# Recurrence of a Trainium2 kernel: levels 2 to 5 of the triangular inverse on half of the columns

## The reference, cut to what matters

```
def _wkv_step(S, inp):
    r_t, w_t, k_t, v_t, a_t, b_t = inp
    sa = jnp.einsum('zbhvk,zbhk->zbhv', S, a_t)
    S = S * w_t[..., None, :] + sa[..., :, None] * b_t[..., None, :] + v_t[..., :, None] * k_t[..., None, :]
    return S, jnp.einsum('zbhvk,zbhk->zbhv', S, r_t)

def wkv_bidir(state0, scan_in):
    state, ys = lax.scan(_wkv_step, state0, scan_in)
    ys = jnp.moveaxis(ys, 0, 2)
    return state, ys[0] + ys[1][:, ::-1]
```

## Time and profile before

| | before |
|---|---|
| three runs | 4251.36, 4251.43, 4254.16 us (median 4251.43) |
| the profiled execution, first to last instruction | 4251.6 us |
| PE busy over the span | 3519.7 us (83%) |
| DVE, ACT, POOL busy | 1262.1, 816.8, 419.9 us |
| mean granted TensorE clock over the span | 0.907 |
| the stretch of the 24 rounds, 1853.3 to 2652.5 us | 799.2 us |
| in it, PE, DVE, ACT, POOL busy | 634.95, 425.37, 354.89, 292.31 us |
| in it, mean granted TensorE clock | 0.91 |

### The profile page before, as it was taken

One profiled execution on the slowest core, in us unless ns is written; L12 is line 12 of the kernel. 1 busy time (PEld: TensorE's weight loads), 2 busy tenths in 40 slices (PEclk: granted clock), 3 DMA queues, 4 the chain that ended last, 5 costly groups with the idle time before them and its releaser, 6 DMA issues. The chain is left out here.

```text
span 4251.6 us, 104941 instructions
## 1 busy us (share of the span) xinstructions
PE 3519.7 (83%) x46600; PEld 2194.1 (52%) x46600; DVE 1262.1 (30%) x2938; ACT 816.8 (19%) x1925; POOL 419.9 (10%) x466
## 2 busy tenths in 40 slices
PE   4999995999997169967877877669999946998987
PEld 2445544555554135546666667345555523464564
DVE  2131114111111440045555555541111112053263
ACT  1011001110000100034444443010000001152152
POOL 0000000000000100033333333000000000000000
PEclk7999996999998589969899899769999978999998
DMA  7741115899998432110000000359999973211110
GB/s 271 297 172 40 55 40 209 302 393 389 384 385 314 154 87 98 57 38 16 18 18 18 18 18 9 123 201 336 391 382 386 384 267 94 92 40 32 59 41 25
DMA packets 319424, 707.15 MB, mean 166 GB/s; under 512 B 26829, under 2 KB 74925, under 8 KB 318348
## 3 DMA queue, kind: packets, MB, share of 16 engines
q1 hardware_dynamic: 268036, 613.55, 39.0%
q0 software_dynamic: 13552, 46.49, 3.5%
q10 hardware_dynamic: 37400, 40.52, 2.7%
HBM read 648.20 MB, written 52.31 MB: 165 GB/s over the span
## 5 line engine op out<-in xcount | busy, mean ns | idle before, releaser
L906 PE MATMUL banks<-w_gate_up,x_turned 128*32 128x256 f32 x12288 | 697.9, 383 | 31.1 <-DMA w_gate_up<-in_moe_w_up_dram 29.7
L906 PEld LDWEIGHTS banks<-w_gate_up,x_turned 128*32 128x32 f32 x12288 | 409.7, 111 | 287.8 <-issue 46.4
L924 PE MATMUL banks<-w_down_ring,hidden_turned 128*32 128x256 f32 x6144 | 344.8, 380 | 0.0
L987 DVE TENSOR_TENSOR hidden<-silu_gate,banks 128x128 f32<-128x128 f32 x192 | 55.3, 288 | 766.2 <-ACT silu_gate L961 766.2
L924 PEld LDWEIGHTS banks<-w_down_ring,hidden_turned 128*32 128x32 f32 x6144 | 193.7, 110 | 128.0
L341 PE MATMUL banks<-const_cols,h_tokens 128*128 128x128 f32 x240 | 53.7, 402 | 234.1 <-DVE h_tokens L314 151.1
L878 POOL DMA_INDIRECT x_rows<-h_rows,cell_index x64 | 58.4, 912 | 1862.9 <-PE banks L898 993.3
L460 PE MATMUL banks<-gmlp_weights,h_turned_gmlp 128*128 128x512 f32 x384 | 174.2, 609 | 12.2 <-DMA gmlp_weights<-in_ga_w_in_dram 12.2
L961 ACT ACTIVATE silu_gate<-banks 128x128 f32<-128x128 f32 x192 | 53.3, 278 | 670.2 <-PE banks L906 670.2
L2053 POOL TENSOR_TENSOR l_quarters<-l_rows,scan_masks 128x256 f32<-128x256 f32 x240 | 146.8, 646 | 249.9 <-ACT l_rows L1973 249.9
L341 PEld LDWEIGHTS banks<-const_cols,h_tokens 128*128 128x128 f32 x240 | 45.3, 216 | 243.2 <-DVE h_tokens L314 158.2
(11 more groups left out here) (469 smaller groups left out, 5348.1 us busy)
## 6 DMA issues: line engine op xcount, KB each, us to landing
w_gate_up<-in_moe_w_gate_dram SPq DMA_DIRECT2D x70, 2048.0 KB, 20.4
w_gate_up<-in_moe_w_up_dram SPq DMA_DIRECT2D x70, 2048.0 KB, 24.7
w_down_ring<-in_moe_w_down_dram SPq DMA_DIRECT2D x70, 2048.0 KB, 21.4
u_channels<-in_ada_w_dram SPq DMA_DIRECT2D x40, 1024.0 KB, 6.8
y_rows<-y_out_rows ACTq DMA_DIRECT2D x256, 96.0 KB, 6.1
gmlp_weights<-in_ga_w_in_dram SPq DMA_DIRECT2D x8, 2048.0 KB, 8.2
ab_weights<-in_ab_w_in_dram SPq DMA_DIRECT2D x6, 2048.0 KB, 8.5
ada_first<-in_ada_w_dram SPq DMA_DIRECT2D x2, 4096.0 KB, 17.5
```

The lines of the kernel that those rows point to most:

```text
L906: last = pe.matmul(ps[strip(j), GU + g, 0:2 * FQ].rearrange("p (a c) -> p a c", a=2), xT[:, e % 2, k, strip(g)], wgu[e % 3][:, :, k, j * F ...
L924: last = pe.matmul(ps[strip(j), Y + g // 2, (g % 2) * DQ:(g % 2 + 1) * DQ], hT[:, g, strip(k)], wd[:, e % 2, k, j * DQ:(j + 1) * DQ], star ...
```

## The change

What it does:

1. In levels 2 to 5 a matmul moves only the 32 columns of each unit that can be nonzero in the off-diagonal blocks (`own_half`), where it moved 64. Loads of weights stay 64x64, and the number of matmuls stays. Level 1 keeps 64 columns.
2. ACT copies 128 elements per partition of Z in levels 2 to 5, where it copied 256, into a buffer of that level's own (`Z[n]`, the other half set to zero once, by 8 memsets of 128x256 on DVE ahead of the rounds). Level 1's step now lies in `a_and_mv`.
3. DVE adds 256 elements in levels 2 to 4, where it added 512, and 128 in level 5, where it added 256. Both sides still go in one instruction, with strided operands: runs of 4, 8, 16 and 32 elements at levels 2, 3, 4, 5.
4. X is laid out by direction first, so that the same columns serve the inverse of one direction and the transpose of the other; the masks and the order of the units in `l_rows` follow (`turned`).
5. `y_two_heads` is dropped. ACT writes the transposed Y back into `y_channels`; its wait for the earlier store moves from there to round 1, just ahead of the copy that writes `y_channels` anew, and is then for the store of two groups before.

```diff
         quarter = (at // size == to // size) & (at % size >= size // 2) & (to % size < size // 2)
         turned = (at // size == to // size) & (to % size >= size // 2) & (at % size < size // 2)
-        parts[f"q1_{n}"], parts[f"q0_{n}"] = turned, quarter
-        if n == 0:
-            parts["x0"], parts["x1"] = quarter, turned
+        parts[f"q0_{n}"], parts[f"q1_{n}"] = quarter, turned
...
     def on_scalar(self, act):
         self.wait(act, "y_turned", 1)
-        self.wait_before(act, "y_stored")
...
-        XI, XX, Z = two("inverse_of_pairs", [P, 2, 4, CHUNK]), two("inverse_both_ways", [P, 2, 4, CHUNK]), two("step", [P, 4, CHUNK])
+        XI, XX = two("inverse_of_pairs", [P, DIRS, 2, 2, CHUNK]), two("inverse_both_ways", [P, DIRS, 2, 2, CHUNK])
+        Z = {n: two(f"step{n}_", [P, 4, CHUNK]) for n in range(2, LEVELS)}
+        Z[1] = [AM[h][:, 0:2, :, :].rearrange("p u a c -> p (u a) c") for h in range(2)]
...
+        half = CHUNK // 2
+        turned = lambda z, ti: (1 - z) * 2 + ti
+        def own_half(ap, zz, n):
+            return ap.rearrange("p (b a s) -> p b a s", a=2, s=2 ** n)[:, :, zz, :]
+        def own_halves(ap, n, apart, width):
+            s = 2 ** n
+            return bass.AP(tensor=ap.tensor, offset=ap.offset, ap=[ap.ap[0], [apart + s, DIRS], [2 * s, width // (2 * s)], [1, s]])
+        packed = lambda ap, n: ap.rearrange("p (z b s) -> p z b s", z=DIRS, s=2 ** n)
...
-                            for u in range(4):
+                            for u, (z, ti) in enumerate(units):
                                 for cc in range(2):
-                                    last = pe.matmul(ps[from_row(h, cc), 4 * h + 1, u * CHUNK:(u + 1) * CHUNK], LQ[h][to_row(h, cc), n - 1, u, :],
-                                                     X[h][to_row(h, cc), 0, u, :], start=True, stop=True)
+                                    factor, x = LQ[h][to_row(h, cc), n - 1, turned(z, ti), :], X[h][to_row(h, cc), z, 0, ti, :]
+                                    if n == 1:
+                                        last = pe.matmul(ps[from_row(h, cc), 4 * h + 1, u * CHUNK:(u + 1) * CHUNK], factor, x, start=True, stop=True)
+                                    else:
+                                        sums = ps[from_row(h, cc), 4 * h + 1, u * half:(u + 1) * half].rearrange("p (b s) -> p b s", s=2 ** n)
+                                        last = pe.matmul(sums, factor, own_half(x, z, n), start=True, stop=True)
...
                                     if n < last_lv:
-                                        pe.matmul(ps[to_row(h, cc), 4 * h, u * CHUNK:(u + 1) * CHUNK], X[h][here, 1, u, :], Z[h][here, u, :], start=True, stop=True)
-                                    last = pe.matmul(ps[here, 4 * h + 1, (4 + u) * CHUNK:(5 + u) * CHUNK], Z[h][here, u, :], X[h][here, 1, u, :], start=True, stop=True)
+                                        pe.matmul(sums(to_row(h, cc), 0, own), x, own_half(step, z, n), start=True, stop=True)
+                                    last = pe.matmul(sums(here, 1, other), step, own_half(x, 1 - z, n), start=True, stop=True)
...
+                            elif n < last_lv:
+                                x = own_halves(XX[h][:, 0, 0, 0, :], n, 4 * CHUNK, 4 * CHUNK)
+                                sums = ps[:, 4 * h:4 * h + 2, 4 * CHUNK:6 * CHUNK].rearrange("p a (z c) -> p z a c", z=DIRS)
+                                step = dve.tensor_tensor(x, sums, x, ALU.add)
                             else:
-                                sums = ps[:, 4 * h + 1, high]
-                                flat = lambda X: X[h][:, 1, :, :].rearrange("p u c -> p (u c)")
-                            DVE.mark(dve.tensor_tensor(flat(XX), sums, flat(XI if n == 1 else XX), ALU.add), by_dve, f"XX{n}_{h}")
+                                x = own_halves(XX[h][:, 0, 1, 0, :], n, 4 * CHUNK, 2 * CHUNK)
+                                step = dve.tensor_tensor(x, packed(ps[:, 4 * h + 1, 4 * CHUNK:6 * CHUNK], n), x, ALU.add)
+                            DVE.mark(step, by_dve, f"XX{n}_{h}")
...
-                            ACTS.mark(copy(Z[h][:, :, :].rearrange("p u c -> p (u c)"), ps[:, 4 * h + 1, low]), by_act, f"Z{n}_{h}")
+                            if n == 1:
+                                step = copy(Z[n][h][:, :, :].rearrange("p u c -> p (u c)"), ps[:, 4 * h + 1, low])
+                            else:
+                                step = copy(own_halves(Z[n][h][:, 0, :], n, 2 * CHUNK, 2 * CHUNK), packed(ps[:, 4 * h + 1, 0:2 * CHUNK], n))
+                            ACTS.mark(step, by_act, f"Z{n}_{h}")
...
                     need("YC")
+                    if rnd == 1 and c >= 2:
+                        act.wait_ge(scan_s["y_stored"], 16 * (c - 1))
```

More of the change, by code:

```diff
@@ L1723, in recurrence @@
         prepare = [Prepare(room, prepare_s, c, sets[c % 2]) for c in range(KD)]
-        scan = [Scan(core, c, scan_s, outs[c % 2], state, f_whole, y_tokens, y_dram, 3 if c < KD - 1 else 7) for c in range(KD)]
+        scan = [Scan(core, c, scan_s, outs[c % 2], state, f_whole, y_dram, 3 if c < KD - 1 else 7) for c in range(KD)]
         nothing = iter(())
@@ L1778, in _ @@
                     wait(by_dve, DVE, "QG", 1)
-                    for u, (z, ti) in enumerate(units):
+                    for z, ti in units:
+                        u = turned(z, ti)
                         for h, cc in quads:
@@ L1810, in _ @@
                             wait(by_act, ACTS, f"Z{n}_{h}")
-                            for u in range(4):
+                            for u, (z, ti) in enumerate(units):
                                 for cc in range(2):
-                                    here = from_row(h, cc)
+                                    here, x, step = from_row(h, cc), X[h][from_row(h, cc), 1 - z, 1, ti, :], Z[n][h][from_row(h, cc), u, :]
+                                    own, other = z * 2 + ti, (1 - z) * 2 + ti
+                                    if n == 1:
+                                        pe.matmul(ps[to_row(h, cc), 4 * h, own * CHUNK:(own + 1) * CHUNK], x, step, start=True, stop=True)
+                                        last = pe.matmul(ps[here, 4 * h + 1, (4 + other) * CHUNK:(5 + other) * CHUNK], step, x, start=True, stop=True)
+                                        continue
+                                    sums = lambda rows_, side, q: ps[rows_, 4 * h + side, 4 * CHUNK + q * half:4 * CHUNK + (q + 1) * half].rearrange("p (b s) -> p b s", s=2 ** n)
                                     if n < last_lv:
-                                        pe.matmul(ps[to_row(h, cc), 4 * h, u * CHUNK:(u + 1) * CHUNK], X[h][here, 1, u, :], Z[h][here, u, :], start=True, stop=True)
-                                    last = pe.matmul(ps[here, 4 * h + 1, (4 + u) * CHUNK:(5 + u) * CHUNK], Z[h][here, u, :], X[h][here, 1, u, :], start=True, stop=True)
+                                        pe.matmul(sums(to_row(h, cc), 0, own), x, own_half(step, z, n), start=True, stop=True)
+                                    last = pe.matmul(sums(here, 1, other), step, own_half(x, 1 - z, n), start=True, stop=True)
                             PE.mark(last, products, f"XX{n}_{h}")
@@ L1856, in _ @@
                     wait(by_act, ACTS, "MV")
-                    for u in range(4):
+                    for u, (z, ti) in enumerate(units):
                         for h, cc in quads:
                             here = from_row(h, cc)
-                            last = pe.matmul(ps[row[cc], 4 * h + 1, u * P:(u + 1) * P], XX[h][here, 1, u, :],
+                            last = pe.matmul(ps[row[cc], 4 * h + 1, u * P:(u + 1) * P], XX[h][here, 1 - z, 1, ti, :],
                                              AM[h][here, u, :, :].rearrange("p a c -> p (a c)"), start=True, stop=True)
@@ L1922, in _ @@
                         dve.wait_ge(by_act, ACTS.of(f"L_{h}", R))
[L1923 removed]
+                        DVE.mark(dve.copy_predicated(XI[h][:, :, 1, :, :], both("q0_0", 2, CHUNK).bitcast(U32), by_dir(fours(ps[:, 4 * h, low]))),
                                  by_dve, f"XM_{h}")
```

20 lines of the change are left out of this document (12 added, 8 removed).

## The result

The changed kernel takes 4352.66 us (median of four runs, 4343.39 to 4360.23) against 4252.8 (4251.36 to 4254.69) for the kernel before: 1.0225 times, 95% interval 1.0204 to 1.0245. It is about 100 us slower; forecast were +64, with 4315 us.

A forecast was written before the change was run, and what follows sets the result against it. No engine is full, PE is nearest; a round is a hand-over-hand chain. Sum: 4251.6 - 9.7 (copies) - 6.6 (additions) + 0 (PE's pace) + 80 (clock) = 4315.3 us; range 4205 to 4390.

The forecast's parts named there:

- A: In the 24 rounds the clock falls further than now: 4315 us, own range 4275 to 4370; chance 0.54.
- ACT's copies: Levels 2 to 5: 192 copies shorten by 110 ns each; 71 PE waits shorten by 136 ns each, -9.7 us.
- DVE's additions: Levels 2 to 5: shorter additions, mostly under PE's other work; waits before L1860 and L1800 shrink, -6.6 us.
- PE's pace: Levels 2 to 5: loading weights, not columns, sets the matmul pace, so 32 columns save 0.
- The clock, +80: In the rounds, fewer columns keep the clock low: 200 us more at 1.2 GHz, at 0.40 each, +80 us.
- Rival C: Levels 2 to 5: columns set PE's pace after all, saving up to 92 us of matmul time; 4181 us, chance 0.12.
- B: In the rounds the clock holds at 0.91 and only shorter copies and additions count: 4235 us, chance 0.20.
- D: In the rounds gain and clock loss cancel, or strides eat the gain: 4243 to 4260 us, chance 0.14.
- The memsets, the new wait, the masks and the layout: Ahead of and within the rounds: memsets fit into slack, the awaited store is old, sizes stay; 0 us.

The follow-up runs named there:

- the run with 96: Changed kernel with 96 columns moved in levels 2 and 3 of round 0, 64 elsewhere in levels 2 to 5: 4243.1 us against 4254.0, 0.9972 times the kernel before.
- the second measurement: The changed kernel, unaltered, timed again beside the experiments: 4341.43 us against 4254.0, 1.0195 times the kernel before.
- the first run: Changed kernel, but TensorE moves its 32 columns twice (64) in levels 2 to 5: 4254.21 us against 4261.76, 0.9983 times the kernel before.

## Why the prediction was right, and where it was off

**Direction and mechanism: right.** It named the clock as the one large term and the place, rounds 0 first. The time, 4353, is inside the range, and inside A's own.

**ACT's copies, -9.7, and DVE's additions, -6.6: right as waits, too large at the end.** The run with the clock restored has 16.7 us less of these waits, 7.4 on ACT and 9.3 on DVE; the sum had 16.3 (2.7 of it for shorter matmuls, which that run does not have). But it gains only 7 us (2 to 13), at a mean clock like that of before. The sum took every wait as time on the path, and about half of it shows at the end. Whether the rest was never on the path or is spent by another part of the change, no run tells.

**PE's pace, 0: right.** 1.12 against 1.15 us at 2.4 GHz, and 1.92 against 1.97 at 1.2. Rival C is out. (By the prediction's own working the router's pace is 0.21 us and not 0.20; nothing hangs on it.) TensorEngine Tiling (Array Packing) of the Trainium skill, section Performance Considerations, puts a matmul of one column level with one of 60; the trace agrees for 32 against 64 columns, and the run with 96 shows that the flat part ends before that: 1.54 us.

**The clock, +80: the step that was mis-sized.** The text had 200 us more at 1.2 GHz, at 0.40. The trace shows 321 more (141 to 462). By the growth of the stretch they cost 0.32 to 0.35 each: 94.7 us, with the 7 us of relief that reach the end or with all 16.7 of the shorter waits. That is +102 to +111 in place of +80. Of the two parts, rounds 0 had 144 and show 172 (131 to 303); near, by the mechanism as described, with falls of 37 us where the text had 35. Rounds 1 and 2 had 56 (a fall in every third of them, 10 us each) and show 148: all sixteen have some time at 1.2 GHz now, where before only two had. The length was about right, 20 falls with 158 us in all; their number was not. I had taken PE's waits in rounds 1 and 2 as mostly harmless, since they did no harm at 64 columns; the runs with columns back in round 0 alone (159 us at 1.2 GHz in rounds 1 and 2) and in rounds 1 and 2 alone (21 us) show that it was the 64 columns around these waits that made them so.

The experiments with narrow matmuls show 0.30 to 0.45 us for each us at 1.2 GHz, worked out in the same way: 0.30 where rounds 1 and 2 are narrow ((828.5 - 801.4 + 16.7) / (288 - 141)), 0.42 where rounds 0 are. All executions of the second measurement, and not only the profiled one, give the same: their mean clocks, 0.875 and 0.907, make some 290 us more at 1.2 GHz, for 87 us and the 7 of relief, 0.32 each. The Trainium skill's page TensorE: Matmul & The Clock Gate, section HAM oscillation — how this bites in real kernels, charges each such microsecond with half a microsecond; by that the 321 us would have cost 160, which the 102 to 111 us of the stretch contradict.

The rows of the changed fourth round 0 show PE busy without a gap for 29.9 us (levels 2 to 5) at 0.50, and the run that differs in moved columns alone brings the clock back. The same page of the Trainium skill, section What's actually happening, says that the clock follows how busy PE has lately been; busy as the profile counts it, that is not borne out here.

**Rivals B and D** assumed that the clock would hold, or nearly. B's place in the experiments is the first run, where it does hold: 0.9983. **The memsets, the new wait, the masks and the layout, 0:** all of them are in that run as well, and it is faster than the kernel before. They cost at most what its shorter waits give and its end does not show, some 9 us; they were not taken apart.

**What stays open.** Why rounds 1 and 2 lose the clock at some waits and not at others; whether it is the columns moved or the columns written that count; where the other half of the shorter waits went; and how much of the last 16 us gained would be there with 96 columns in the kernel before, which has no free columns in the bank of level 2 and was not tried.

## What to carry to other kernels

Before making matmuls narrower, look whether the columns set their time (a run of the same weights with fewer and with more columns). If they do not, the cut saves next to nothing on TensorE, and the columns may be what holds its clock: look for stretches in which PE is 100% busy at a granted clock of 0.50, and ask what is moved in them. A copy that nobody reads, in the groups right behind a fall of the clock, can be worth more than the work it adds (0.9948 and 0.9963 here, against 0.9983 with 64 columns); the same copy also where the clock is up took the gain away again (0.9998).

## What the runs showed of the hardware that was not expected

- With 64*64 weights and two quarters of the array at work, 32 and 64 columns take nearly the same time at 2.4 GHz (1.12 and 1.15 us for 32 matmuls) and at 1.2 GHz (1.92 and 1.97 us). The router row had suggested the latter for full-size weights only.
- The clock stayed at 0.50 through 37.7 us in which PE was busy for 37.5 (the last four pieces of the changed round); with twice the columns it was at 1.00 from level 3 on.
- The cost is not in proportion to the columns taken away. Of the 11 narrow groups of a round, the 5 of levels 4 and 5 cost 0.1%, the 6 of levels 2 and 3 cost 1.7% over the run with all back; in rounds 0 what matters is whether the clock is down when they start.
- In rounds 1 and 2 narrow matmuls let the clock fall where it was up: 148 us more at 1.2 GHz with the change, 20 falls where there were 2. With 64 columns the same places held it (21 us).
- Operands in strided runs of 4 to 32 elements cost DVE and ACT nothing: 424 and 291 ns, and 277 ns, where dense ones took 425, 288 and 275.
